# A decoder layer's last output run: final norm weights multiplied in ahead, last unit by token tile, row scaling on two engines, eight stores

## The reference

```python
hf = rmsnorm(x, norm_ffn_g[l])
gt, up = jnp.split(hf @ w_ffn_in[l], 2, axis=-1)
x = x + (jax.nn.silu(gt) * up) @ w_ffn_out[l]
return rmsnorm(x, norm_final_g)      # x * rsqrt(mean(x*x) + eps) * g
```

## Time and profile before

| What | Value |
|---|---|
| median of 3 runs (lowest, highest) | 2829.58 us (2829.12, 2830.18) |
| the profiled execution: time, span | 2829.69 us, 2827.9 us |
| busy share PE, DVE, ACT, POOL | 98%, 72%, 37%, 20% |
| instructions of PE, DVE, ACT, POOL | 16311, 3061, 1788, 471 |
| mean granted TensorE clock | 0.997 of full speed |

### The profile page before, as it was taken

How to read it: one execution, slowest core, us unless ns; L and a number is a source line. 1 busy time by engine, 2 the same in 40 slices (tenths; PEclk the granted TensorE clock), 3 DMA queues, 4 the chain that set the end, 5 groups by cost and what they waited for, 6 DMA issues and landing times.

```text
span 2827.9 us, 42359 instructions
## 1 busy us (share of the span) xinstructions
PE 2769.9 (98%) x16311; PEld 2444.3 (86%) x16311; DVE 2037.4 (72%) x3061; ACT 1044.8 (37%) x1788; POOL 561.8 (20%) x471
## 2 busy tenths in 40 slices
PE   7999999999999999999999999999999999999997
PEld 6888778888888888888778999999999999788886
DVE  6544476676655555655678888888888888888887
ACT  6201254444420322211144444444444444443334
POOL 0100033343320555411000122122212221010000
PEclk9999999999999999999999999999999999999999
DMA  7532333323333445544334455555565557999882
GB/s 233 165 96 75 76 84 94 94 75 84 85 99 103 108 122 151 146 112 111 90 127 133 121 144 149 164 145 145 148 166 142 148 145 259 295 290 311 285 264 94
DMA packets 528678, 415.62 MB, mean 147 GB/s; under 512 B 12420, under 2 KB 472056, under 8 KB 522616
## 3 DMA queue, kind: packets, MB, share of 16 engines
q1 hardware_dynamic: 509680, 381.85, 45.6%
q0 software_dynamic: 5344, 10.49, 2.3%
q10 hardware_dynamic: 13480, 20.91, 2.2%
HBM read 354.22 MB, written 58.98 MB: 146 GB/s over the span
## 4 chain that ended last, share of the span: by engine, by line
PE 85%; DVE 6%; ACT 3%; DMA 2%; issue 2%; POOL 1%; ACTq 0%; DVEq 0%; POOLq 0%; SPq 0%
PE banks L870 12%; PE banks L872 12%; PE banks L871 12%; PE banks L1260 10%; PE banks L1259 10%; PE banks L1258 10%; PE banks L1319 4%; PE banks L1321 4%; PE banks L1320 4%; PE banks L1033 1%; PE banks L1090 1%; PE banks L1092 1%; PE banks L1091 1%; PE banks L1064 1%; PE banks L1049 1%
## 5 line engine op out<-in xcount | busy, mean ns | idle before, releaser
L1336 DVE CAST w_hi<-raw 128x512 fp32r<-128x512 f32 x424 | 230.3, 543 | 363.0 <-PE banks L872 297.8
L870 PE MATMUL banks<-act_hi,w_hi 128*128 128x512 f32 (+1 forms) x1232 | 489.1, 397 | 0.4 <-ACT gates L2017 0.4
L871 PE MATMUL banks<-act_lo,w_hi 128*128 128x512 f32 (+1 forms) x1232 | 481.1, 390 | 0.0
L872 PE MATMUL banks<-act_hi,w_lo 128*128 128x512 f32 (+1 forms) x1232 | 480.9, 390 | 0.0
L1258 PE MATMUL banks<-t_hi,wf_hi 128*128 128x256 f32 x1312 | 371.3, 283 | 0.0
L1259 PE MATMUL banks<-t_lo,wf_hi 128*128 128x256 f32 x1312 | 371.3, 283 | 0.0
L1260 PE MATMUL banks<-t_hi,wf_lo 128*128 128x256 f32 x1312 | 371.3, 283 | 0.0
L1338 DVE TENSOR_TENSOR w_lo<-raw,w_hi 128x512 fp32r<-128x512 f32 x424 | 318.0, 750 | 14.6
L1259 PE MATMUL banks<-tok_lo,wf_hi 128*128 128x256 f32 x984 | 278.5, 283 | 0.0
L1260 PE MATMUL banks<-tok_hi,wf_lo 128*128 128x256 f32 x984 | 278.5, 283 | 0.0
L1258 PE MATMUL banks<-tok_hi,wf_hi 128*128 128x256 f32 x984 | 278.5, 283 | 0.0
(11 more groups left out here) (317 smaller groups left out, 5640.8 us busy)
## 6 DMA issues: line engine op xcount, KB each, us to landing
raw_f<-in_w_ffn_in_dram SPq DMA_DIRECT2D x82, 1024.0 KB, 8.8
...
```

Source lines behind the costliest of these rows:

```text
L870: pe.matmul(dst, w_hi[:, q, j, 0:m], hi, start=first, stop=False)
L871: pe.matmul(dst, w_hi[:, q, j, 0:m], lo, start=False, stop=False)
L872: return pe.matmul(dst, w_lo[:, q, j, 0:m], hi, start=False, stop=last)
L1336: dve.tensor_copy(w_hi[:, q, :, 0:width], src).then_inc(hi_done, 1)
```

## The change

Four things are changed, all in the last run and behind it.

GpSimd multiplies columns 0 to 1023 of each token tile by the final norm's weights, in the order 2, 3, 0, 1, each 128x1024, once the first sums of squares are taken (`squared` at 2 for tiles 2 and 3, at 4 for tiles 0 and 1, above its base).

The last product of the last run, j = 6, is ordered by token tile: TensorE does all of tile 0 first, with the weights of both granules, and then all of tile 1. It therefore waits for the second granule's `wo_lo` in the middle of the first (`f_lo >= g + 2`). VectorE evacuates each tile's bank by itself (`last_rows`, 128x512).

The scaling of a tile is split: ScalarE scales columns 0 to 1023 (one factor per token, the weights are in already), VectorE multiplies columns 1024 to 2047 by factor and weights. Tiles 2 and 3 share one factor step, tiles 0 and 1 have one each. The squares of columns 1024 to 2047 of tiles 0 and 1 become one 128x1024 instruction each, taken after `last_rows`.

SP issues eight stores of half a tile (0.5 MB) where it issued four.

```diff
+        KEPT = 2 * len(BY_ACT)
+        GAINED = (2, 3, 0, 1)
+        ROWS_OF = (slice(2, 4), slice(0, 1), slice(1, 2))
@@ sync
-            for n, c in enumerate((2, 3, 0, 1)):
-                sp.wait_ge(y_done, n + 1)
-                sp.dma_start(out_v[:, c], acc[:, c]).then_inc(stored, 16)
-            sp.wait_ge(stored, 16 * TC)
+            for done, value, c, h in ((acc_kept, KEPT + 1, 2, 0), (acc_kept, KEPT + 2, 3, 0), (y_done, 1, 2, 1), (y_done, 2, 0, 1),
+                                      (acc_kept, KEPT + 3, 1, 0), (y_done, 3, 1, 1), (acc_kept, KEPT + 4, 0, 0), (y_done, 4, 3, 1)):
+                sp.wait_ge(done, value)
+                sp.dma_start(out_v[:, c, h * D // 2:(h + 1) * D // 2], acc[:, c, h * D // 2:(h + 1) * D // 2]).then_inc(stored, 16)
+            sp.wait_ge(stored, 16 * 8)
@@ tensor
-                for k in range(2):
-                    for t in range(2):
+                whole = cb == len(OUT_RUNS) - 1 and j == 6
+                steps = [(n, k, q) for n in range(2) for k in range(2)] if whole else [(q, k, n) for k in range(2) for n in range(2)]
+                for x, k, t in steps:
+                    if whole and (q, x, k) == (0, 1, 0):
+                        pe.wait_ge(f_lo, g + 2)
@@ vector
-            def finish_rows(c, th):
-                dve.wait_ge(rstd_done, 1 + 2 * (2 - th))
+            def last_rows(t):
+                b = bank_of(LAST, 6)
+                dve.wait_ge(f_unit, unit_end(LAST, 6) - 1 + t)
+                dve.tensor_tensor(acc[:, t, 3 * OF:4 * OF], acc[:, t, 3 * OF:4 * OF], banks[:, b + t], EVAC[6][2]).then_inc(banks_read, 1)
+            def finish_rows(c):
+                dve.wait_ge(rstd_done, (5, 7, 3, 3)[c])
                 dve.wait_ge(final_g_landed, 16)
-                dve.scalar_tensor_tensor(out=acc[:, c], in0=acc[:, c], scalar=y_scale[:, c:c + 1], in1=final_g_bc[:],
-                                         op0=ALU.mult, op1=ALU.mult).then_inc(y_done, 1)
+                dve.scalar_tensor_tensor(out=acc[:, c, D // 2:D], in0=acc[:, c, D // 2:D], scalar=y_scale[:, c:c + 1],
+                                         in1=final_g_bc[:, D // 2:D], op0=ALU.mult, op1=ALU.mult).then_inc(y_done, 1)
...
-                    finish_scale(1)
-                if cb == LAST and (j, q) == (6, 1):
-                    finish_rows(2, 1)
-                    finish_rows(3, 1)
-            evacuate(LAST, 6)
-            finish_scale(0)
-            finish_rows(0, 0)
-            finish_rows(1, 0)
+                    finish_scale(0)
+            last_rows(0)
+            finish_rows(2)
+            finish_scale(1)
+            last_rows(1)
+            finish_rows(0)
+            finish_scale(2)
+            finish_rows(1)
+            finish_rows(3)
@@ scalar
+            def finish_rows(c):
+                act.wait_ge(rstd_done, (5, 7, 3, 3)[c])
+                act.wait_ge(final_gained, 1 + GAINED.index(c))
+                act.activation(acc[:, c, 0:D // 2], acc[:, c, 0:D // 2], ACT.Copy, scale=y_scale[:, c:c + 1]).then_inc(acc_kept, 1)
...
-                    finish_root(1)
-                    act.wait_ge(*read_at(LAST, 5))
-                    for c in (0, 1):
-                        square(c, 2 * OF, OF, 1)
-            act.wait_ge(*read_at(LAST, 6))
-            for c in (0, 1):
-                square(c, 3 * OF, OF, 2)
-            finish_root(0)
+                    finish_root(0)
+                    finish_rows(2)
+                    finish_rows(3)
+            done, value = read_at(LAST, 6)
+            for c in range(2):
+                act.wait_ge(done, value + c)
+                square(c, 2 * OF, 2 * OF, 1)
+                finish_root(1 + c)
+            finish_rows(1)
+            finish_rows(0)
@@ gpsimd
+            pool.wait_ge(final_g_landed, 16)
+            for c in GAINED:
+                pool.wait_ge(squared, 2 * DK + (2 if c > 1 else 4))
+                pool.tensor_tensor(acc[:, c, 0:D // 2], acc[:, c, 0:D // 2], final_g_bc[:, 0:D // 2], ALU.mult).then_inc(final_gained, 1)
```

More of the change, by code:

```diff
@@ L528, in build @@
         y_done = sem("y_done")
+        final_gained = sem("final_gained")
         stored = sem("stored")
@@ L1313, in _ @@
                 h = (h_full if c else h_first)[j]
-                for k in range(2):
-                    for t in range(2):
-                        dst = bank[bank_of(cb, j) + t]
-                        hi, lo = (h[:, 2 * q + k, w, t * P:(t + 1) * P] for w in range(2))
-                        last = k == 1 and q == halves_of(cb) - 1
-                        pe.matmul(dst, hi, wo_hi[g % 3][:, k], start=STARTS[j] and q == 0 and k == 0, stop=False, skip_group_check=True)
-                        pe.matmul(dst, lo, wo_hi[g % 3][:, k], start=False, stop=False, skip_group_check=True)
-                        mm = pe.matmul(dst, hi, wo_lo[g % 3][:, k], start=False, stop=last, skip_group_check=True)
+                whole = cb == len(OUT_RUNS) - 1 and j == 6
[3 more added lines that the diff above has]
+                        pe.wait_ge(f_lo, g + 2)
+                    dst = bank[bank_of(cb, j) + t]
+                    w = (GRAN0[cb] + j * halves_of(cb) + x) % 3
+                    hi, lo = (h[:, 2 * x + k, w2, t * P:(t + 1) * P] for w2 in range(2))
+                    first, last = x == 0 and k == 0, k == 1 and x == halves_of(cb) - 1
+                    pe.matmul(dst, hi, wo_hi[w][:, k], start=STARTS[j] and first, stop=False, skip_group_check=True)
+                    pe.matmul(dst, lo, wo_hi[w][:, k], start=False, stop=False, skip_group_check=True)
+                    mm = pe.matmul(dst, hi, wo_lo[w][:, k], start=False, stop=last, skip_group_check=True)
                 mm.then_inc(f_unit, 1)
@@ L1805, in add_rest, with finish_scale @@
                 a.then_inc(rest_added, 1)
-            def finish_scale(th):
-                dve.wait_ge(squared, 2 * DK + 4 + 4 * (2 - th))
-                dve.tensor_reduce(ss[:, 2 * th:2 * th + 2], y_part[:, 2 * th:2 * th + 2], AX.X, ALU.add).then_inc(summed, 1)
-                dve.wait_ge(norm_root, 5 - th)
-                dve.reciprocal(y_scale[:, 2 * th:2 * th + 2], ss[:, 2 * th:2 * th + 2]).then_inc(rstd_done, 1)
-                dve.wait_ge(rstd_done, 1 + 2 * (2 - th) - 1)
-                dve.wait_ge(norm_inv, 3)
-                dve.tensor_tensor(y_scale[:, 2 * th:2 * th + 2], y_scale[:, 2 * th:2 * th + 2], rstd[:, 2 * th:2 * th + 2], ALU.mult).then_inc(rstd_done, 1)
-            def finish_rows(c, th):
-                dve.wait_ge(rstd_done, 1 + 2 * (2 - th))
+            def finish_scale(n):
+                rows = ROWS_OF[n]
+                dve.wait_ge(squared, 2 * DK + (8, 9, 10)[n])
+                dve.tensor_reduce(ss[:, rows], y_part[:, rows, 0:2 if n else 3], AX.X, ALU.add).then_inc(summed, 1)
+                dve.wait_ge(norm_root, 4 + n)
+                dve.reciprocal(y_scale[:, rows], ss[:, rows]).then_inc(rstd_done, 1)
+                dve.wait_ge(rstd_done, 2 + 2 * n)
+                dve.wait_ge(norm_inv, 3)
+                dve.tensor_tensor(y_scale[:, rows], y_scale[:, rows], rstd[:, rows], ALU.mult).then_inc(rstd_done, 1)
+            def last_rows(t):
[4 more added lines that the diff above has]
+                dve.wait_ge(rstd_done, (5, 7, 3, 3)[c])
                 dve.wait_ge(final_g_landed, 16)
-                dve.scalar_tensor_tensor(out=acc[:, c], in0=acc[:, c], scalar=y_scale[:, c:c + 1], in1=final_g_bc[:],
-                                         op0=ALU.mult, op1=ALU.mult).then_inc(y_done, 1)
+                dve.scalar_tensor_tensor(out=acc[:, c, D // 2:D], in0=acc[:, c, D // 2:D], scalar=y_scale[:, c:c + 1],
+                                         in1=final_g_bc[:, D // 2:D], op0=ALU.mult, op1=ALU.mult).then_inc(y_done, 1)
             LAST = len(OUT_RUNS) - 1
```

6 lines of the change are left out of this document (3 added, 3 removed).

## The result

The changed kernel took 2835.11 us (median of 22 runs, 2831.92 to 2836.97), the kernel before 2830.98 us (22 runs beside them, 2829.12 to 2834.12). The ratio is 1.0015, with a 95% interval of 1.0009 to 1.0021: slower by 4.1 us, and the interval excludes no change. The profiled execution took 2835.48 us, its span is 2833.7 us. Predicted were 2833.9 us, on a kernel before of 2829.6; the difference of 4.3 us was predicted for the one of 4.1.

What follows compares the result with a forecast made beforehand. TensorE took 85% of the span, fed in the last run by a VectorE-ScalarE ring without slack; -3.4 + 0 + 7.1 + 0.6 = +4.3 us on 2829.69 gave 2834.0, as median 2833.9 us; range 2829.5 to 2837.5.

Steps and rivals of the forecast that it cites:

- the ring of VectorE and ScalarE: Last run: VectorE sums weight blocks, ScalarE rounds, VectorE subtracts; no slack, so VectorE's losses between 2787 and 2799 reach TensorE.
- Term 3: Last run: GpSimd's four multiplications take turns with VectorE's two-SBUF-input instructions and delay the end by 7.1 us.
- Term 1: Behind the last run: split scaling and half-tile stores end the engines 4.7 us earlier and the span 3.4 us earlier.
- Term 2: j = 6 of the last run: TensorE's order by token tile, with a wait of 0.24 us, costs 0.
- Term 4: Behind 2806 in the last run: TensorE loses its full clock after its waits, +0.6 us, bounds 0 and +1.1.
- The waits of TensorE: Last run: TensorE idle 2.7 us before granule (3,1), 1.8 before (4,0) and 2.9 before (4,1).
- it does what it says: Rival, chance 0.07: GpSimd's instructions in the last run delay nobody, leaving -3.4 us, 2826.2 us.
- VectorE keeps its place: Rival, chance 0.10: in the last run GpSimd gets in only when VectorE pauses, costing near 3.8 us; time 2830.0 us.
- The clock that stays at half: Rival, chance 0.25: TensorE's clock stays at half well behind 2806; with 8 us at half, +7.1 us, 2836.7 us.

Runs made afterwards that it cites:

- gain_only: The kernel before with GpSimd's four multiplications added and VectorE's finish waiting for them: 2837.97 us against 2830.36, ratio 1.0025.
- memset: As no_gain, but GpSimd writes zeros into unused buffers at the places of its four multiplications, reading nothing: 2827.36 us against 2830.36, ratio 0.9990.
- one_read: The changed kernel with GpSimd multiplying by the constant 1, one operand read instead of two: 2827.55 us against 2830.77, ratio 0.9989.
- no_gain: The changed kernel without GpSimd's four multiplications and without ScalarE's wait for them: 2828.38 us against 2830.36 for the kernel before, ratio 0.9993.
- pieces: The changed kernel with each GpSimd multiplication cut in two of 512 columns, still released by the squares alone: 2832.72 us against 2830.66, ratio 1.0007.

## Why the prediction was right, point by point

*What bounds the kernel.* That the ring of VectorE and ScalarE has no slack in the last run held: 3.5 to 3.6 us more on each of ScalarE's two waits became waits of TensorE, and in gain_only a `wo_lo` of (4,1) that is 7.15 late ends the span 7.2 late.

*Term 3, GpSimd's multiplications: +7.1 predicted, +7.13 measured* (`wo_lo` of (4,1) in the changed kernel, +7.15 in gain_only). Every step of the working can be laid beside the rows: shifted, the four VectorE rows end at 2790.11, 2793.45, 2800.34 and 2803.66, where 2790.0, 2793.35, 2800.25 and 2803.6 were predicted. The constant 0.1 is GpSimd's start 0.15 behind the squares. Its own 2.38 us, the 2.25 behind a VectorE row and the 1.09 behind GpSimd came out as taken from much shorter instructions. The Trainium skill (SBUF — State Buffer, "Who interferes with whom") says that such a VectorE instruction contends with a GpSimd instruction that reads SBUF, not with one that only writes, and that the later one blocks fully. The changed kernel and memset agree (3.42 against 1.22 us). one_read agrees that the two contend, but not that the whole instruction blocks: of 2.78 us some 1.0 held VectorE.

*Term 1, the end: -3.4 predicted, -3.2 measured* (no_gain). The engines' part was -4.7 predicted and -4.4 measured: the factor chains took 0.2 to 0.3 longer than added up. The stores came out 0.15 us better: from the last row to the end of the span 5.65 us in no_gain, against 5.8. The packets of 4 KB, priced at nothing, cost 3 to 4%, some 0.2 us on the last 2 MB. The prediction's upper bound for them mixes two units: 2.53 us is for 1.05 MB (a quarter of 4.19), 3.38 us for 1 MB, so +1.7 should have been +2.0; the forecast used neither. The runs also take the term apart: without the order by token tile the end is 2.0 later, without the eight stores 2.5, each taken away by itself. These do not add up to 3.2, and the scaling on two engines was not run alone.

*Term 2, TensorE's order: 0 predicted.* The wait in the middle of (6,0) was to be 0.24 us; TensorE ended 0.26 later than in the old order. VectorE was to come for tile 0 at 2810.55, which is where no_gain has it, shifted, and it waits for nothing there.

*Term 4, the clock: +0.6 predicted.* In the first profile of the changed kernel the sum of the parts is 7.13 - 4.40 = 2.73 and the last row is 3.36 late: 0.63 for the clock. In the second profile the clock does not fall and the row is 2.75 late: 0.0. The 0.6 was a value between the bounds 0 and 1.1 that I could not place, so that the first profile has 0.63 is luck, as the second shows; in pieces the fall cost 0.9. With the fall TensorE started its last matmul 1.05 us later (shifted) than without it, of which the cover (time that TensorE can lose there before VectorE has to wait for it) took 0.4.

*The waits of TensorE:* 2.7, 1.8 and 2.9 predicted; 2.65, 1.54 and 2.66 in the second profile. *From TensorE's end to the span's end:* 11.5 predicted, 11.1 and 11.6 in the two profiles.

*The sum* was +4.3; the profiles have +4.5 and +3.9, the medians +4.1 and +4.4. The absolute 2833.9 is 1.2 us below the measured median because it was set on a profiled 2829.69, while 22 runs of the same kernel have a median of 2830.98. Three runs were too few to place the kernel before within 1 us.

*The rivals.* GpSimd's instructions do delay VectorE, so "it does what it says" is out; its 3.4 us below before is nearly what the end gives without them (no_gain: 3.2 by the profile, 2.0 by the medians). "VectorE keeps its place" is out by gain_only and by pieces, where both take turns throughout. The clock that stays at half was not seen: the fall lasted from 2807.4 to 2810.1 in one profile and was absent there in the other. What was said for it, that the trace before nowhere has three waits in a row, is a misreading: the 14 us of rows 5 have four (1.82, 0.33, 1.12 and 1.13 us), though none as long as the 2.65 here.
